# Twelve or eight fetch buffers for expert rows in the later part of two layers

## The reference

```python
def one(hb):                      # 128 tokens
    q = (hb @ p["peer_wq"]).reshape(PEER_TOKEN_BLOCK, PEER_HEADS, 2, PEER_QDIM // 2)
    s = jnp.einsum("thsd,hskd->thsk", q, p["peer_keys"])
    s_top, i_top = lax.top_k(s, PEER_TOPK)
...
    experts = e1 * PEER_KEYS + e2
    gates = jax.nn.softmax(g_score, axis=-1)
    u = jnp.take(p["peer_u"], experts, axis=0)
    act = jax.nn.gelu(jnp.einsum("thkd,td->thk", u, hb), approximate=False) * gates
    v = jnp.take(p["peer_v"], experts, axis=0)
    return jnp.einsum("thk,thkd->td", act, v)
```

## Time and profile before

| | |
|---|---|
| Median of 3 runs | 4248.29 us (4245.42 to 4248.42) |
| Span of the profiled execution | 4241.7 us |
| Median less that span | 6.6 us |
| PE busy | 3056.6 us (72%) |
| DVE busy | 2864.0 us (68%) |
| POOL busy | 1564.1 us (37%) |
| ACT busy | 1196.1 us (28%) |
| HBM read | 1473 MB, 349 GB/s over the span |

### The profile page before, as it was taken

The page is one execution under the profiler, slowest core; times in us unless marked ns, Lnnn a source line. Parts: engine busy times, 40 slices in busy tenths (PEclk is TensorE's granted clock), DMA queues, the critical chain, the costliest instruction groups (busy, mean ns, idle before and its releaser), DMA issues. The chain is left out here.

```text
span 4241.7 us, 37585 instructions
## 1 busy us (share of the span) xinstructions
PE 3056.6 (72%) x11918; PEld 1283.3 (30%) x11918; DVE 2864.0 (68%) x7196; ACT 1196.1 (28%) x3224; POOL 1564.1 (37%) x1352
## 2 busy tenths in 40 slices
PE   8999899766677755555566677999867655655555
PEld 4655444322222211111122222565322211111111
DVE  2426847899888897555555665666888998555555
ACT  2125423323223222111222343563322322111111
POOL 0002213454444454444344442002454554444443
PEclk9999999878888877778788888999988877767777
DMA  4114859999999999999999997106999999999998
GB/s 178 44 37 180 304 208 356 409 421 417 421 420 395 421 421 420 421 421 416 421 418 420 417 414 294 40 1 263 419 420 420 420 417 416 420 420 420 421 421 356
DMA packets 234010, 1481.23 MB, mean 349 GB/s; under 512 B 26060, under 2 KB 37548, under 8 KB 63572
## 3 DMA queue, kind: packets, MB, share of 16 engines
q0 software_dynamic: 184320, 1342.26, 76.5%
q1 hardware_dynamic: 48116, 132.61, 8.5%
q10 hardware_dynamic: 1376, 3.96, 0.2%
HBM read 1473.31 MB, written 5.42 MB: 349 GB/s over the span
## 5 line engine op out<-in xcount | busy, mean ns | idle before, releaser
L2205 PE MATMUL banks<-arena 128*64 128x512 f32 x5104 | 1653.5, 808 | 1135.8 <-ACT arena L2469 1080.1
L1914 POOL DMA_INDIRECT arena<-experts,arena x1280 | 1504.3, 1175 | 2206.0 <-PE banks L2205 1541.8
L2648 DVE CUSTOM_DVE_ANT_0 arena<-arena 128x1024 f32<-128x1024 f32 x1280 | 1539.8, 1224 | 845.5 <-DMA arena<-experts,arena 845.2
L2205 PEld LDWEIGHTS banks<-arena 128*64 128x64 f32 x5104 | 454.0, 184 | 2252.0 <-ACT arena L2469 1251.6
L2463 ACT ACTIVATE arena<-arena 128x4 f32<-128x4 f32 x319 | 65.9, 206 | 2275.4 <-DVE arena L2648 2275.3
L2469 ACT ACTIVATE arena<-arena 128x64 f32<-128x64 f32 x1276 | 339.3, 336 | 37.7 <-ACT arena L2463 1.2
L2007 PE MATMUL banks<-arena 128*128 128x512 f32 (+3 forms) x960 | 287.4, 453 | 0.8 <-DVE arena L2554 0.7
L453 PE MATMUL banks<-arena 128*128 128x512 f32 (+1 forms) x640 | 208.6, 486 | 1.9 <-ACT arena L514 1.9
L2007 PEld LDWEIGHTS banks<-arena 128*128 128x128 f32 x960 | 160.0, 190 | 108.4 <-issue 88.8
L1934 PE MATMUL banks<-arena 128*128 128x512 f32 x416 | 186.7, 596 | 7.1 <-DMA arena<-l_w_out 3.9
L453 PEld LDWEIGHTS banks<-arena 128*128 128x128 f32 x640 | 120.5, 190 | 86.3 <-issue 77.7
(11 more groups left out here) (273 smaller groups left out, 3034.0 us busy)
## 6 DMA issues: line engine op xcount, KB each, us to landing
arena<-l_w_ada SPq DMA_DIRECT2D x48, 1024.0 KB, 8.3
arena<-wq SPq DMA_DIRECT2D x54, 512.0 KB, 7.9
arena<-experts,arena POOLq DMA_INDIRECT x1280, 17.5
arena<-l_w_in SPq DMA_DIRECT2D x6, 2048.0 KB, 7.9
arena<-l_w_out SPq DMA_DIRECT2D x4, 1536.0 KB, 14.1
arena<-l_w_o SPq DMA_DIRECT2D x4, 1024.0 KB, 8.5
arena<-keys SPq DMA_DIRECT2D x27, 128.0 KB, 10.9
arena<-gates SPq DMA_DIRECT2D x6, 512.0 KB, 12.5
```

The source lines that it names most:

```text
L1914: pool.indirect_dma_start(slots[n], None, tbl, bass.IndirectOffsetOnAxis(ap=expert[:, ring[c], k:k + 1], axis=0)).then_inc(land[n]["sem"], ...
L2205: mm = pe.matmul(core["ps"][QS * j:QS * j + QS, c, :], diag[:, g % 2, k, :], v[:, D + c * 512:D + (c + 1) * 512], start=(g % (NB * PH) == ...
L2648: dve.tensor_tensor_reduce(u, u, rep[i // PH % 2][:, k % NQ, :], 1.0, 0.0, ALU.mult, ALU.add, dots[:, k:k + 1]).then_inc(dot["sem"], up(dot))
```

## The change

The map of each layer gets an entry `narrow`: a fetch number and a set of slots. From fetch 480 of layer 0 (position 120) and fetch 256 of layer 1 (position 64) on, the slots 6, 7, 8 and 9 are left out of the ring, and the fetches go around the eight that remain (0 to 5, 10 and 11). The slot of a fetch is found as the next one in the ring after that of the fetch before. `BATCH` is 4 before and after. Nothing is put into the memory that is left unused.

```diff
--- before.py
+++ after.py
@@ -1520,7 +1520,7 @@
      "choose_from": 14, "early": 7, "ahead": 6, "asked_from": 12, "spread_at": (1, 2), "spread_first": (14, 15),
      "halves": ((0, 0), (0, 1)) + tuple((t, 0) for t in range(1, 6)) + tuple((t, 1) for t in range(1, 6)),
      "opening": tuple(range(4)) * 4 + (4, 5, 6, 0, 1, 2, 3) * 5 + (4,), "ready": 4, "column": (4, 5, 6),
-     "near": 2, "halved": range(2, PH),
+     "near": 2, "halved": range(2, PH), "narrow": (BATCH * 120, (6, 7, 8, 9)),
      "g1": L0 + 15360, "g2": L0 + 17408,
      "diag": L0 + 18432, "wq": L0 + 19968, "sc": L0 + 22016, "keys": L0 + 24064,
      "rep": (L0 + 3072, L0 + 5120), "ht": HO,
@@ -1533,7 +1533,7 @@
               [(h, t) for h in range(4) for t in range(1, 4)] + [(h, t) for t in range(2, 4) for h in range(4, PH)],
      "choose_from": 3, "early": 2, "ahead": 4, "asked_from": 3, "spread_at": (4, 5), "spread_first": (4, 5),
      "halves": tuple((t, c) for t in range(TL) for c in range(2)),
-     "opening": tuple(range(8)) * 2, "ready": 8, "column": (), "near": 2, "halved": (),
+     "opening": tuple(range(8)) * 2, "ready": 8, "column": (), "near": 2, "halved": (), "narrow": (BATCH * 64, (6, 7, 8, 9)),
      "w": RO + SLOT, "g1": HO + 16384, "g2": HO + 17408,
      "diag": HO + 18432, "wq": XO + TL * D, "sc": HO + 19968, "keys": HO + 21504,
      "rep": (HO + 22528, HO + 24576), "ht": HO + 26624,
@@ -1608,9 +1608,16 @@
     slots = [view(core, o, ROWS) for o in m["slots"]]
     NS = len(slots)
     slot_of, before, used = {}, {}, {}
+    ring_of = list(range(NS))
     for u in range(steps * TOPK):
         n = u - len(m["opening"])
-        slot_of[u] = m["opening"][u] if n < 0 else (n + 1 + max(m["opening"])) % NS
+        if u == m["narrow"][0]:
+            ring_of = [r for r in range(NS) if r not in m["narrow"][1]]
+        if n < 0:
+            slot_of[u] = m["opening"][u]
+        else:
+            later = [r for r in ring_of if r > slot_of[u - 1]]
+            slot_of[u] = later[0] if later else ring_of[0]
         before[u] = used.get(slot_of[u], (0, None))
         used[slot_of[u]] = (before[u][0] + 1, u)
     x = view(core, XO, TT, D)
```

## The result

| | before | after |
|---|---|---|
| Median | 4246.9 us (4 runs, 4245.4 to 4248.4) | 4371.6 us (4 runs, 4365.0 to 4374.4) |
| Ratio | | 1.0293 (95% interval 1.0281 to 1.0305) |
| Span of the profiled execution | 4241.7 us | 4371.3 us |

The kernel is slower by 124.8 us, 2.9%. The forecast was 4286 with a range up to 4345, so the direction was right and the size more than three times what I had forecast.

What follows compares the result with a forecast made beforehand. The prediction took the DMA transfers of expert fetches as the bound. Layer 1's 18 us, layer 0's 14 and tile additions' 6 summed to 38 us: a span of 4280 and a median of 4286 us, range 4250 to 4345.

Steps and rivals of the forecast that it cites:

- What bounds the kernel, the period, the holding time: Expert fetches: DMA transfers bound the kernel; 9.94 us per four fetches, buffers held 6.65 us from landing to next issue.
- In the narrow ring the queue isn't empty: Eight-buffer stretches: issue starts 3.3 us before the previous landing, so part of the 3.8 us start may hide.
- The size a batch: Narrow ring at PE's low clock: a 20.39 us loop plus long issues costs 0.29 us a batch, bounds 0 and 0.82.
- Layer 0: 70 batches from position 120 at 0.29 us, times two thirds because PE often has its full clock: 14 us.
- Tile additions: Four, at positions 128 and 160 of layer 0, 64 and 96 of layer 1: 1.6 us exposed each, 6 us.
- behind POOL's wait there are only later fetches: Narrow stretches: DVE waits for those landings, ACT for DVE, PE for ACT; nothing else of weight stands between the engines.
- (b): Rival: each narrow-ring batch pays a queue restart of 0.82 us, +91 us, 4340 us; chance 0.22 including +60 to +102.
- (a): Rival: transfers stay the bound, only tile additions and long issues cost, 0 to +8 us, about 4252; chance 0.24.
- (d): Rival: the diff doesn't do what it says; the prediction found no such place and gave no chance.
- The formula of the Trainium skill: One fetch takes 2.0 us plus bytes / 436 GB/s, 4.4 us for 1 MiB; loop 19.5 us, no loss.
- The signs that I named: Narrow-stretch profile: latency 11 to 14 us, layer 1 period 10.2 us, rate about 403 GB/s; period 10.8 would mean (b).

Runs made afterwards that it cites:

- two in flight: Kernel before with twelve buffers, but from positions 120 and 64 POOL issues a fetch only when the fetch two before it has landed: 4735.9 us, 1.1154.
- three in flight: Kernel before with twelve buffers, but from positions 120 and 64 POOL allows at most three fetches issued and not yet landed: 4422.1 us, 1.0415.
- half the sums: Changed kernel with columns 0 to 511 of PE's sums left out in the narrow stretches, so the output lacks them: 4278.2 us, 1.0071 of before.
- PE at its full clock: Changed kernel with 18 small, unread PE matmuls after each batch's sums in layer 1 from position 66 on: 4351.2 us, 1.0248 of before.
- four in flight: Kernel before with twelve buffers, but from positions 120 and 64 POOL allows at most four fetches issued and not yet landed: 4245.6 us, 1.0000.
- ten buffers without 4 and 5: Changed kernel with only two buffers left out from the same positions, 4 and 5 in layer 0, 8 and 9 in layer 1: 4246.4 us, 1.0001 of before.

## Why the prediction was wrong

**What bounds the kernel, the period, the holding time.** Right: 9.94 us a batch while the queue is full, 6.65 us from landing to issue, the issue 3.3 us ahead of the landing (3.2 in the batch shown, 4.2 in the median, as the period grew). No step on PE, ACT or DVE became the bound.

**The step that failed** is "In the narrow ring the queue isn't empty": that an issue done 2.35 us ahead of the last landing "lacks little or nothing", because a fetch needs 4.6 us from the end of its issue, of which 2.485 are transfer. I measured the queue by its landings. But a landing waits for the slowest of the sixteen engines, and half of them are through with the fetch 1.8 us before it (median in layer 1; eleven by 2.1 us before it in the batch above). An issue that starts 3.3 us ahead and is done 2.3 us ahead, with 0.7 us more to its first packet, finds them dry. (In the median of layer 1 it was done 2.9 us ahead, since the longer period gives some room back.) The 4.6 us are true of a fetch in a short queue, as two in flight show; they aren't the time within which a fetch keeps the queue running. With three in flight the issue is done 3.7 us ahead, that is 1.6 us earlier than 4.6 us of latency would demand (4.6 - 2.5 = 2.1 us), and each fetch still loses 0.35 us.

**The size a batch.** I took 0.29 us, from four fetches issued to an idle queue (13.74 us). Part of the start was to hide behind the batch before. Instead the four took longer than in an idle queue: 15.45 us from the first issue to the fourth landing (median in layer 1; 15.6 in the batch above). With 6.67 us of holding time the loop is 22 us, 11 a batch. Layer 1 lost 59.6 us over 62 batches, 0.96 each; the term was 18 us and measured 60. I had bounded it by 0.82, the distance of two landings after an empty queue, which was too low as well: of the first fetches that came late the mean distance was 3.80 us, not 3.30. The packets show a part of this: one of 8 KB takes 0.314 us in the mean in layer 1's stretch before, 0.333 in the changed kernel and 0.369 with two in flight. Why packets are slow after a pause, and why the engines are out of step, isn't shown by the runs.

**Layer 0.** The term was 14 us and measured 57, 0.81 us for each of 70 batches. The discount of a third for PE's full clock rested on "the loop is 18.6 us and costs nothing". With a loop of 22 us, 1.8 us less are 20.2, still over 19.88: where the holding time was 1.7 us shorter (half the sums), 12 of the 60 us of layer 1 stayed, and where it was 1.2 us shorter (PE at its full clock) some 40. In the changed kernel's layer 0 only a fifth of the batches were held less than 5.3 us; the median is 6.67 there too. So the discount came out as a sixth and not a third.

**Tile additions.** 6 us for four of them; the runs don't separate them.

**The late load.** Not in my sum: 8 us. I had written that behind POOL's wait there are only later fetches, and didn't follow the other reader of the table, SP's wait for the last use of buffers 4 and 5. Ten buffers with and without them show it.

**The rivals.** (b), with 91 us, had the right mechanism, a restart of the queue in most batches, and was still short by a quarter of the loss. (a) was the wrong side of the threshold; four in flight shows the state it describes. On (d) I was wrong to find no such place. In layer 0 the diff shifts the ring from fetch 52 on, long before the narrow stretch: the opening ends on buffer 4, and fetch 52 went to buffer 7 and now goes to 5. The traces show the shift in every kernel made from the changed one. It costs nothing by itself: ten buffers without 4 and 5 and four in flight have it too, and measure 1.0001 and 1.0000. The formula of the Trainium skill (DMA: Bandwidth & Descriptors, Anatomy of one DMA — SWDGE path), 4.4 us for such a transfer, agrees with the 4.6 us measured for single fetches; by it the ring would have cost nothing, and the measurement, 125 us, decides. A time for one transfer doesn't tell how many have to be under way.

**The signs that I named.** The latency was to fall from 17.5 to 11 to 14 us and was 9.4 in layer 1 (median). The period of 10.8 that I had given as the sign of (b) was nearest: it was 10.9 to 11.0.

## What to carry to other kernels

Before a ring of buffers is cut, ask how far ahead of the previous landing the next transfer's issue is done; for these 1 MB gathers 5.4 us was enough and 3.5 us was not, though a single one lands 4.6 us after its issue. If a loop is short by a microsecond or two, releasing buffers in smaller groups can buy it: pairs instead of fours gave back all but 3 to 6 of 125 us. Follow every reader of the slot table: a buffer whose memory is wanted next should be the first to leave the ring.

## What the runs showed of the hardware

The DMA share of a window hides a queue that is too short. In layer 1 it stood at 0.97 with 371 and 382 GB/s and at 1.01 with 420, because the packets of a restarting queue take longer (thirteen of the first ones, in the batch above, 0.74 to 1.13 us instead of 0.31): a loss of 9 to 12% in the rate shows as 4% in the share. The rate has to be read.

A landing is no sign that the engines have just stopped. It follows the last of a fetch's 16 small packets by 0.37 us (median in the changed kernel's layer 1), but half of the 16 have come 1.8 us before it. With two in flight that is only 0.6 us: with so short a queue the engines stay together. POOL starts an issue 0.76 us after the landing that it waits for (two, three and four in flight alike).

The threshold is narrow. From two to three to four fetches in flight the cost over the 524 fetches was 489, 175 and 0 us, and with eight in a fixed ring of two batches 125 us, since there the four of one batch are issued together and the queue runs short between batches.
